# Layer kernel: the sums of squares of the first layer norm, split into two float32r parts and added in two passes, in halves of 172 columns

## The reference

```
x1 = LayerNorm(ALPHA * x + concat(A, B) @ w_out)
x2 = LayerNorm(ALPHA * x1 + square(relu(x1 @ w_ff1 + b_ff1)) @ w_ff2 + b_ff2)

def _layer_norm(x, g, b):
    mu = mean(x); xc = x - mu
    var = mean(xc * xc)
    return xc * rsqrt(var + 1e-5) * g + b
```

## Time and profile before

| | us |
|---|---|
| median of 3 runs | 1048.4 (1048.13 to 1048.55) |
| the profiled execution | 1048.17 |
| its span, first to last instruction | 1046.6 |
| PE busy | 1036.3 |
| VectorE busy | 747.9 |
| ScalarE busy | 495.6 |
| GpSimd busy | 101.6 |

### The profile page before, as it was taken

How to read it: one execution, slowest core, us unless ns; L and a number is a source line. 1 busy time by engine, 2 the same in 40 slices (tenths; PEclk the granted TensorE clock), 3 DMA queues, 4 the chain that set the end, 5 groups by cost and what they waited for, 6 DMA issues and landing times. The chain is left out here.

```text
span 1046.6 us, 19119 instructions
## 1 busy us (share of the span) xinstructions
PE 1036.3 (99%) x7761; PEld 1023.6 (98%) x7761; DVE 747.9 (71%) x1034; ACT 495.6 (47%) x711; POOL 101.6 (10%) x140
## 2 busy tenths in 40 slices
PE   9999999999999999999999999999999999999997
PEld 9999999999899999999999999999999999999986
DVE  6795775535797596876766767768766677887977
ACT  6554534345533576664664564565443323334223
POOL 3112221020211000000000000000000000000027
PEclk9999999999999999999999999999999999999999
DMA  9546996165224215245455445499634415325304
GB/s 283 144 176 153 246 199 135 61 165 126 71 102 141 102 41 216 98 142 185 129 157 185 141 153 183 148 296 344 229 122 166 159 62 182 122 93 172 122 3 160
DMA packets 97780, 159.95 MB, mean 153 GB/s; under 512 B 6485, under 2 KB 52277, under 8 KB 96681
## 3 DMA queue, kind: packets, MB, share of 16 engines
q1 hardware_dynamic: 88290, 127.72, 37.9%
q0 software_dynamic: 9152, 30.79, 11.3%
q10 hardware_dynamic: 270, 0.49, 0.2%
HBM read 111.56 MB, written 53.29 MB: 158 GB/s over the span
## 5 line engine op out<-in xcount | busy, mean ns | idle before, releaser
L2623 PE MATMUL bank<-x_hi,w_hi 128*128 128x344 f32 (+1 forms) x696 | 227.5, 327 | 0.2 <-DVE x_lo L1774 0.2
L2623 PE MATMUL bank<-x_hi,d_lo 128*128 128x258 f32 x968 | 222.4, 282 | 0.0
L2623 PE MATMUL bank<-x_lo,w_hi 128*128 128x344 f32 (+1 forms) x696 | 222.0, 319 | 0.0
L2623 PE MATMUL bank<-x_hi,w_lo 128*128 128x344 f32 x528 | 168.7, 319 | 0.0
L2623 PEld LDWEIGHTS bank<-x_hi,d_lo 128*128 128x128 f32 x968 | 165.7, 189 | 0.0
L2623 PEld LDWEIGHTS bank<-x_hi,w_hi 128*128 128x128 f32 (+1 forms) x696 | 130.4, 187 | 1.0 <-DVE x_lo L1774 0.5
L2623 PEld LDWEIGHTS bank<-x_lo,w_hi 128*128 128x128 f32 (+1 forms) x696 | 130.2, 187 | 0.4
L2623 PE MATMUL bank<-x_hi,s_hi 128*128 128x258 f32 x352 | 99.5, 283 | 0.0
L2623 PE MATMUL bank<-x_lo,s_hi 128*128 128x258 f32 x352 | 99.3, 282 | 0.0
L2623 PEld LDWEIGHTS bank<-x_hi,w_lo 128*128 128x128 f32 x528 | 99.2, 188 | 0.0
L2623 PE MATMUL bank<-t_hi,s_hi 128*128 128x258 f32 x336 | 95.2, 283 | 0.0
(11 more groups left out here) (463 smaller groups left out, 2570.7 us busy)
## 6 DMA issues: line engine op xcount, KB each, us to landing
h_ops<-h_unit SPq DMA_DIRECT2D x56, 258.0 KB, 7.3
x_lo_raw<-h_ops SPq DMA_DIRECT2D x14, 1032.0 KB, 5.3
s_raw<-in_w_ff SPq DMA_DIRECT2D x14, 1024.0 KB, 6.9
x_lo_raw<-h_ops SPq DMA_DIRECT2D x14, 774.0 KB, 4.5
d_raw<-in_w_ff SPq DMA_DIRECT2D x9, 1024.0 KB, 7.9
w_raw<-in_w_in SPq DMA_DIRECT2D x16, 512.0 KB, 7.1
h_ops<-t_out SPq DMA_DIRECT2D x28, 258.0 KB, 7.6
d_raw<-in_w_ff SPq DMA_DIRECT2D x8, 768.0 KB, 6.4
```

What stands on the lines that cost most here:

```text
L2623: return nc.tensor.matmul(out, lhsT, rhs, start=start, stop=stop, skip_group_check=True)
```

## The change

- Three tiles are added: SSQH (the high part of SSQ, float32r, in the place behind r_std), SSQL (the low part, written over SSQ itself) and ONESR (the ones as float32r, written over the ones by one ScalarE Copy ahead of the first squares).
- ScalarE, in root(b): once the sum is there, it copies SSQ to SSQH, 128x344. Then the square root in two halves of 172 columns, each waiting for its own product.
- GpSimd: for each block two subtractions of 172 columns, SSQL = SSQ - SSQH. They stand ahead of its waits for the storing of x1.
- PE, in square_sums(b): in place of one float32 product of 344 columns, for each half a wait for its low part, then two float32r products of 172 columns, high and low, added up in PSUM. The halves lie in two banks, D_ and T_.
- The counts of two semaphores follow: var_ready and ln_sqrt go up by two in a block.

```diff
+        SSQL = at("square_sum_lo", [P, BLK], R["sample_C"], F32R)
+        SSQH = at("square_sum_hi", [P, BLK], R["r_std"], F32R)
+        ONESR = at("ones_r", [P, P], R["ones"] - 4 * P, F32R)
...
+        SQ_BANK = [D_[:, 0:BLK // 2], T_[:, 0:BLK // 2]]
...
+        def sq_half(x):
+            return slice(BLK // 2 * x, BLK // 2 * (x + 1))
...
+            for b in range(NBLK):
+                pool.wait_ge(ssq_hi, b + 1)
+                for x in range(2):
+                    G.tensor_tensor(SSQL[:, sq_half(x)], SSQ[:, sq_half(x)], SSQH[:, sq_half(x)].bitcast(F32),
+                                    ALU.subtract).then_inc(ssq_lo, 1)
+
             pool.wait_ge(xv_ready, KC * NBLK)
...
             def root(b):
-                act.wait_ge(var_ready, VAR0 + b + 1)
+                act.wait_ge(sq_sum, 5 * b + 5)
+                A(SSQH[:, :], SSQ[:, :], ACT.Copy).then_inc(ssq_hi, 1)
                 if b:
                     act.wait_ge(ln_norm, 2 * b)
-                A(RSTD[:, :], D_[:, 0:BLK], ACT.Sqrt, scale=1.0 / D, bias=EPSC).then_inc(ln_sqrt, 1)
+                for x in range(2):
+                    act.wait_ge(var_ready, VAR0 + 2 * b + x + 1)
+                    A(RSTD[:, sq_half(x)], SQ_BANK[x], ACT.Sqrt, scale=1.0 / D, bias=EPSC).then_inc(ln_sqrt, 1)
...
+            A(ONESR[:, :], ONES[:, :], ACT.Copy)
             square(0, 0, 6)
...
                     if m0 == 7 and b:
-                        dve.wait_ge(var_ready, VAR0 + b)
+                        dve.wait_ge(var_ready, VAR0 + 2 * b)
...
             def r_std(b):
-                dve.wait_ge(ln_sqrt, b + 1)
+                dve.wait_ge(ln_sqrt, 2 * b + 2)
...
             def square_sums(b):
-                pe.wait_ge(sq_sum, 5 * b + 5)
                 if b:
-                    pe.wait_ge(ln_sqrt, b)
+                    pe.wait_ge(ln_sqrt, 2 * b)
                 else:
                     pe.wait_ge(nat_read, 2)
-                mm(D_[:, 0:BLK], ONES[:, :], SSQ[:, :]).then_inc(var_ready, 1)
+                for x in range(2):
+                    pe.wait_ge(ssq_lo, 2 * b + x + 1)
+                    mm(SQ_BANK[x], ONESR[:, :], SSQH[:, sq_half(x)], True, False)
+                    mm(SQ_BANK[x], ONESR[:, :], SSQL[:, sq_half(x)], False, True).then_inc(var_ready, 1)
```

More of the change, by code:

```diff
@@ L272, in build_layer @@
         sq_sum, ln_sqrt, ln_norm = sem("sq_sum"), sem("ln_sqrt"), sem("ln_norm")
+        ssq_hi, ssq_lo = sem("ssq_hi"), sem("ssq_lo")
         squared, var_ready, ln_rstd = stT_read, stT_ready, colT_read
```

## The result

The median is 1058.6 us (1057.74 to 1059.2, 5 runs) against 1048.4 (1048.13 to 1048.63, 5 runs): a ratio of 1.0098, 95% interval 1.0087 to 1.0109. The change makes the kernel 10.2 us slower. Forecast were 1053.6 us and a range up to 1056.6. The profiled execution took 1057.74 us, its span is 1056.1.

A forecast was written before the change was run, and what follows sets the result against it. PE's stream was taken as the bound, with no later wait to swallow a delay. Losses of 0.6, 2.1 and 2.5 us in blocks 0, 1 and 2 made 5.2: 1053.4 us profiled, 1053.6 as median, range 1050.7 to 1056.6.

The forecast's parts named there:

- pass price: PE, all blocks: a float32r pass of 172 columns costs 0.08 to 0.29 us, 0.18 taken.
- Block 0: First block: PE waits for half 1 and is back 0.35 to 0.8 us later, 0.6 taken.
- If GpSimd comes first: Block 1: GpSimd's half 1 runs ahead of VectorE's next x_lo; loss 1.9 to 2.3 us, 2.1 taken.
- rival B: Block 1: VectorE wins at 369.56, half 1 waits for a second x_lo; sum 7.6 us, 1056.0, chance 0.17.
- Block 2: Third block: Copy waits behind w_hi, GpSimd behind w_lo; PE loses 2.3 to 2.7 us, 2.5 taken.
- discount for PE's arriving later: Block 2: PE arrives 2.7 us later after blocks 0 and 1, so a loss of 3.9 us becomes 2.5.
- Rival C: Blocks 1 and 2: PE's stands bring the clock to 1.2 GHz, 2 to 4 us on top, 1056.5 or so, chance 0.08.
- the next 2 to 4 us: Behind PE's stands: the length of PE work taking twice as long if the clock fell, adding 2 to 4 us.
- GpSimd's exclusion by VectorE: Blocks 1 and 2: GpSimd stands still during VectorE's two-SBUF-input instructions; a select took 1.95 us against 0.65.
- the residual, with one SBUF input, would leave GpSimd alone: Block 1: the residual of 369.14 reads PSUM and one SBUF tile, so it does not hold up GpSimd.

The follow-up runs named there:

- e4_fill: The changed kernel with 22 more unread products of 344 columns on PE ahead of the wait of block 1: 1057.9 us.
- e12_fill_both: The changed kernel with unread products of 344 columns on PE ahead of the waits, 22 in block 1 and 18 in block 2: 1055.5 us.
- e1_one_piece: The changed kernel with each block in one piece of 344 columns (one GpSimd subtraction, two passes in one bank, one sqrt): 1056.7 us.
- e3_no_x_lo: The changed kernel with VectorE's two x_lo of block 0 put behind r_std(1), away from GpSimd's subtractions in block 1: 1057.0 us.

## Why the prediction was wrong

- The bound and the direction held: PE's stream is the time, and the chain ahead of it is a loss. The ends of the pass price (0.08 and 0.29 us) enclosed 0.11; the middle, 0.18, was too high, which made the forecast some 0.15 us a block too slow.
- Block 0: 0.6 forecast, 0.31 measured. Copy (0.49), hand-overs and the 0.56 of a half were right. Half of the difference is the price of the passes; the rest is that the sum ended 1.02 us before PE's last product started (350.56 and 351.58) where it had been 0.83 in the trace before.
- Two steps failed, and block 1 is the first: "If GpSimd comes first", 2.1 us, was the term taken, and it was 3.9 (0.4 of it through the clock). VectorE's x_lo was issued 0.03 us ahead of half 1 and had the port for 1.58 us. That was rival B, given 0.17. With 0.04 us between the two in the forecast's own estimate (369.56 against 369.6) there was no ground to prefer one.
- Block 2: 2.5 forecast, 3.2 measured. The order of events was right (Copy behind w_hi, GpSimd behind w_lo). The discount for PE's arriving later was 0.7 us and not 1.4: the sum was to end 2.1 us before PE came, and ended 1.2 before (388.77 and 390.00). With the first stand longer and the clock low, VectorE stood too (residual at 378.88 waited 3.57 us for PE), and what followed was tied to PE again.
- The clock is the second step: the sum has it at nothing. Rival C had it, with a chance of 0.08 and a price of 2 to 4 us. It cost about 3.1. No row stood behind the forecast's slow work of "the next 2 to 4 us"; measured were some 6 us of work at 0.50, with products 0.28 us apart instead of 0.157. The forecast had PE stand for 1.7 us in block 1 and 2 to 3 in block 2, both of them longer than or as long as any stand in the trace of before, and took the clock as unmoved because no row showed it moving. The stands of 1.27 to 1.36 us in these runs left it up; those of 2.47, 3.23 and 4.33 did not, nor did the 2.11 and 1.40 close behind one another (the change, block 1). A stand of 2.87 left it up (the change, block 2), one of 2.88 did not (e4_fill, block 2). So the length of a stand alone does not decide it, and what else does stays open. TensorE: Matmul & The Clock Gate of the Trainium skill, "What's actually happening", has the throttled clock as what idleness leaves and activity releases; e12_fill_both agrees, 3.1 us won by adding work.
- B and C came together, and the range was made as though only one of them could. B alone, 1056.0, and the measured 3.1 of the clock on top give 1059.1; measured 1058.6. That B's 7.6 us lie so near the 7.4 between the products is luck in part: its block 0 was 0.3 too dear, its block 1 0.3 too cheap.
- GpSimd's exclusion by VectorE held in every run read: 0.56 us beside nothing, 1.96 beside one x_lo, 1.06 for both halves with x_lo away; and VectorE's by GpSimd in e1_one_piece, 1.88 us for an x_lo of 1.58. The Trainium skill has this exclusion in SBUF — State Buffer, "Who interferes with whom"; the rows agree. That the residual, with one SBUF input, would leave GpSimd alone was right too: half 0 of block 1 ended 0.41 us behind x_lo.

## What to carry to other kernels

On an engine that has no idle time, a cheaper instruction is worth its own saving (here 0.13 us three times) and a new hand-over ahead of it costs what of its length the engine has no other work for (undisturbed, stands of 0.8 to 1.36 us in blocks 1 and 2, and 0.1 to 0.3 us lost in block 0, where the sum came early), so count hand-overs first. A helper on GpSimd has to be placed against VectorE's two-input instructions, and a single larger instruction may be safer than two halves, since each is another chance to lose the port. Where a wait of PE is forecast to be longer than any in the trace, the clock belongs into the sum and not among the unlikely rivals, and it adds to whatever made the wait.

## What was not expected of the hardware

- More work made the kernel faster: 40 unused products of 344 columns took 3.1 us off.
- The fall of the clock moves. With the stand of block 1 filled or cut short, it fell in block 2 (e3_no_x_lo, e4_fill; in e1_one_piece in both), so three of the four single edits won 0.7 to 1.9 us where 2.5 to 5 were expected. The change's own profile, with its one fall in block 1, doesn't show this.
- A float32r pass of 172 columns costs 0.11 us behind another, more than half of the 0.157 of 344 columns, and a float32 product of 344 columns 0.58.
